# Two mixers of a four-layer block: heads' norm by four products side by side, the convolution's norm ahead of the scores, weights rounded between the first tiles

## The reference, cut to what matters

```python
xn = rmsnorm(x, norm_mix[l])
proj = xn @ w_in[l]                                   # 1024 -> 2560
u_pool, u_conv, u_diff, u_sc, u_mem = jnp.split(proj, IN_SPLITS, axis=-1)
y_pool = pool_mixer(u_pool, pool_w[l], pool_scale[l])
y_conv = conformer_conv(u_conv, conv_dw[l], conv_ln_g[l], conv_ln_b[l], conv_pw[l])
y_diff = diff_attention(u_diff, diff_qk_norm[l], diff_lambda[l], diff_subln[l], l)
y_sc = short_conv(u_sc, sconv_w[l])
y_mem = memory_attention(u_mem, mem, mem_norm[l], w_mem_kv[l], mem_qk_norm[l])
...
x = x + cat @ w_out[l]                                # cat: the five, each normed
x = x + peer_ffn(rmsnorm(x, norm_ffn[l]), ...)        # 16384 experts, dense here
```

## Time and profile before

| | |
|---|---|
| median of 3 runs | 3377.08 us (3373.78 to 3378.36) |
| profiled execution | 3372.12 us, span 3370.6 us |
| mean granted PE clock | 0.966 |
| PE busy | 3150.4 us, 93% |
| DVE, ACT, POOL busy | 1972.9, 1586.5, 274.8 us (59, 47, 8%) |
| first mixer, from the end of `plain` to the third score products | 1161.8 to 1257.2 us |

### The profile page before, as it was taken

The page is one execution under the profiler, slowest core; times in us unless marked ns, Lnnn a source line. Parts: engine busy times, 40 slices in busy tenths (PEclk is TensorE's granted clock), DMA queues, the critical chain, the costliest instruction groups (busy, mean ns, idle before and its releaser), DMA issues.

```text
span 3370.6 us, 49973 instructions
## 1 busy us (share of the span) xinstructions
PE 3150.4 (93%) x18836; PEld 2673.9 (79%) x18836; DVE 1972.9 (59%) x4121; ACT 1586.5 (47%) x3320; POOL 274.8 (8%) x376
## 2 busy tenths in 40 slices
PE   6998999998899978997999999998899789999999
PEld 3745677776699867986789999988788678999998
DVE  3233433335666556689666666656659876666665
ACT  2254322223655425319555555542541765555554
POOL 0021000000200021008000000001200620000000
PEclk9999999998999988999999999999799999999999
DMA  6502444432155423440455556543144035555554
GB/s 227 178 1 76 156 175 161 166 105 94 45 170 180 156 73 103 152 144 1 157 187 187 186 185 200 182 162 110 56 162 152 30 113 182 187 188 187 184 186 150
DMA packets 135052, 479.82 MB, mean 142 GB/s; under 512 B 15520, under 2 KB 17440, under 8 KB 134048
## 3 DMA queue, kind: packets, MB, share of 16 engines
q1 hardware_dynamic: 132944, 471.26, 42.6%
q10 hardware_dynamic: 1872, 5.38, 0.4%
HBM read 475.53 MB, written 1.05 MB: 141 GB/s over the span
## 4 chain that ended last, share of the span: by engine, by line
PE 88%; DVE 5%; ACT 3%; issue 2%; DMA 1%; POOL 0%; SPq 0%; DVEq 0%; ACTq 0%; POOLq 0%
PE psum L768 15%; PE psum L770 15%; PE psum L769 15%; PE psum L2941 7%; PE psum L2943 7%; PE psum L2942 7%; PE psum L2850 7%; PE psum L2759 4%; PE psum L863 2%; PE psum L1125 2%; PE psum L356 1%; PE psum L1135 1%; PE psum L629 1%; DMA raw<-in_mod_w 1%; DVE a_scaled L733 1%
## 5 line engine op out<-in xcount | busy, mean ns | idle before, releaser
L249 DVE TENSOR_TENSOR w_lo<-raw,w_hi 128x512 fp32r<-128x512 f32 x1424 | 958.4, 691 | 744.9 <-ACT w_hi L240 717.6
L240 ACT ACTIVATE w_hi<-raw 128x512 fp32r<-128x512 f32 x1424 | 864.4, 625 | 795.7 <-PE psum L770 419.3
L768 PE MATMUL psum<-x_hi,w_hi 128*128 128x256 f32 x1968 | 561.2, 285 | 7.7 <-issue 4.2
L770 PE MATMUL psum<-x_hi,w_lo 128*128 128x256 f32 x1968 | 558.2, 284 | 0.0
L769 PE MATMUL psum<-x_lo,w_hi 128*128 128x256 f32 x1968 | 557.7, 283 | 0.0
L2941 PE MATMUL psum<-w_hi,wt_hi 128*128 128x512 f32 x1024 | 406.9, 397 | 6.5 <-DVE wt_lo L3005 6.5
L2943 PE MATMUL psum<-w_hi,wt_lo 128*128 128x512 f32 x1024 | 406.4, 397 | 0.0
L2942 PE MATMUL psum<-w_lo,wt_hi 128*128 128x512 f32 x1024 | 405.8, 396 | 0.0
L768 PEld LDWEIGHTS psum<-x_hi,w_hi 128*128 128x128 f32 x1968 | 373.5, 190 | 17.6 <-issue 9.0
L769 PEld LDWEIGHTS psum<-x_lo,w_hi 128*128 128x128 f32 x1968 | 376.1, 191 | 7.9
L770 PEld LDWEIGHTS psum<-x_hi,w_lo 128*128 128x128 f32 x1968 | 375.1, 191 | 0.0
(11 more groups left out here) (336 smaller groups left out, 4439.0 us busy)
## 6 DMA issues: line engine op xcount, KB each, us to landing
raw<-in_v SPq DMA_DIRECT2D x256, 512.0 KB, 4.4
raw<-in_u SPq DMA_DIRECT2D x190, 512.0 KB, 3.4
raw<-in_mod_w SPq DMA_DIRECT2D x96, 512.0 KB, 4.4
raw<-in_w_gate_up SPq DMA_DIRECT2D x88, 512.0 KB, 5.2
u_raw<-in_u SPq DMA_DIRECT2D x66, 512.0 KB, 3.5
raw<-in_w_in SPq DMA_DIRECT2D x40, 512.0 KB, 3.5
raw<-in_w_down SPq DMA_DIRECT2D x32, 512.0 KB, 3.5
raw<-in_w_peer SPq DMA_DIRECT2D x32, 512.0 KB, 4.2
```

The costliest lines, as they stand in the source:

```text
L240: self.nc.scalar.activation(self.hi[:, m % 4, :], self.half(m), ACT.Copy).then_inc(self.rounded[m % 4], 1)
L249: self.nc.vector.tensor_tensor(self.lo[:, m % 4, :], self.half(m), self.hi[:, m % 4, :], ALU.subtract).then_inc(self.ready[m % 4], 1)
L768: pe.matmul(out[:, 0:width], hi[:, w], x_hi, start=(c == 0), stop=False)
L770: mm = pe.matmul(out[:, 0:width], lo[:, w], x_hi, start=False, stop=(c == total - 1))
```

## The change

The heads' norm becomes a class of its own. The squares of a set of 128x512 are now the moving operand; the weights are 32 columns of 1/n by group (`means`), and the four sets write partitions 0 to 31, 32 to 63 and so on of one bank. One square root on ACT, one reciprocal on DVE of 128x512; then four products over 32 rows each (`back`) spread set s into a bank of its own. The matrices are an input of their own (`head_mats`, 128x192), fetched with the mixer's small tensors. The first turn goes between the two tiles of `mem_values`, the second, in bank 7, behind `second`'s first tile, together with the root. `ln`'s root and inversion go between `third`'s tiles, its spread ahead of the attention's first scores, and its application ahead of the first maxima. ACT and DVE round three halves of `first` behind `plain`'s second tile. The fetch of the mixer's small tensors is now waited for by DVE, POOL and PE. Nothing of the computed values is left out.

```diff
+class HeadNorm:
+    def __init__(self, k, items, mats, banks):
+        self.means, self.back = [mats[:, 0:32], mats[:, 32:64]], mats[:, 64:64 + P]
...
+        self.root = flat(k.spread[:, 0:4, :])
+        self.sums = k.bank[6].use(written=4)
+        self.inv = [k.bank[b].use() for b in banks]
...
+    def scalar_squares(self, after):
+        for s in (0, 2):
+            act.activation(self.k.sq[:, s, :], self.items[s][0], ACT.Square).then_inc(self.by_scalar.sem, 1)
+    def vector_squares(self, after):
+        for s in (1, 3):
+            dve.tensor_tensor(self.k.sq[:, s, :], x, x, ALU.mult).then_inc(self.by_vector.sem, 1)
+    def tensor_sums(self):
...
+        for s in range(4):
+            pe.matmul(use.tensor[self.rows(s), :], self.means[s // 2], self.k.sq[:, s, :], start=True,
+                      stop=True).then_inc(use.written.sem, 1)
+    def scalar_root(self):
+        act.wait_ge(*use.full(4))
+        act.activation(self.root, use.tensor[:], ACT.Sqrt, bias=self.k.eps[:, 0:1]).then_inc(use.read.sem, 1)
+    def vector_invert(self):
+        dve.wait_ge(*self.sums.emptied())
+        dve.reciprocal(self.root, self.root).then_inc(self.inverted.sem, 1)
+    def tensor_spread(self):
...
+        for s, use in enumerate(self.inv):
+            pe.matmul(use.tensor[:], self.back[self.rows(s), :], self.root[self.rows(s), :], start=True,
+                      stop=True).then_inc(use.written.sem, 1)
+    def vector_apply(self):
+        for (x, gain), use in zip(self.items, self.inv):
+            dve.wait_ge(*use.full())
+            dve.scalar_tensor_tensor(out=x, in0=x, scalar=gain, in1=use.tensor[:], op0=ALU.mult,
+                                     op1=ALU.mult).then_inc(use.read.sem, 1)
 class TurnRows:
-    def __init__(self, k, dst, src, n, arrive):
+    def __init__(self, k, dst, src, n, arrive, bank=6):
 class MixerPlain
     def scalar_between(self, n):
+        if n == 1:
+            self.mixer.k.ring.round(0)
     def vector_between(self, n):
+        if n == 1:
+            self.mixer.k.ring.remain(0)
 class MixerMemory
+    def tensor_between(self, n):
+        if n == 0:
+            self.mixer.rows[0].tensor()
+        if n == 1:
+            hold(self.mixer.k.nc.tensor, self.mixer.fetch.done)
+            self.mixer.heads.tensor_sums()
     def scalar_between(self, n):
         self.mixer.k.ring.round(0)
+        if n == 0:
+            self.mixer.rows[0].scalar()
+            self.mixer.heads.scalar_squares(self.mixer.heads_there())
     def vector_between(self, n):
+        if n == 0:
+            self.mixer.heads.vector_squares(self.mixer.heads_there())
         self.mixer.branches.vector_taps(16 + 4 * n, 20 + 4 * n)
         self.mixer.k.ring.remain(0)
 class MixerSecond
+    def tensor_between(self, n):
+        if n == 0:
+            self.mixer.rows[1].tensor()
+    def scalar_between(self, n):
+        if n == 0:
+            self.mixer.rows[1].scalar()
+            self.mixer.heads.scalar_root()
     def vector_between(self, n):
+        if n == 2:
+            self.mixer.heads.vector_invert()
         self.mixer.branches.vector_taps(24 + 2 * n, min(26 + 2 * n, Branches.TAPS))
 class MixerThird
     def scalar_between(self, n):
+        if n == 2:
+            self.mixer.ln.scalar_root()
     def vector_between(self, n):
+        if n == 2:
+            self.mixer.ln.vector_invert()
 class MixerSteps
     def tensor_start(self):
-        self.mixer.ln.tensor_spread()
         self.mixer.branches.tensor()
 class Mixer
+        head_mats = k.sb("head_mats", [P, 64 + P], 137952)
     def tensor(self):
         self.mem_values.tensor()
-        for rows in self.rows:
-            rows.tensor()
-        self.heads.tensor_sums()
         self.second.tensor()
         self.heads.tensor_spread()
         self.third.tensor()
+        self.ln.tensor_spread()
         self.att.tensor()
     def scalar(self):
-        for rows in self.rows:
-            rows.scalar()
-        self.heads.scalar_squares(self.first.done + self.proj_done + self.memory.done + self.mem_values.done)
         self.second.scalar()
-        self.heads.scalar_root()
+        k.warm(ACT.Sqrt)
         self.third.scalar()
         ring.limit = self.beyond()
-        self.ln.scalar_root()
     def vector(self):
-        self.heads.vector_squares(self.first.done + self.proj_done + self.memory.done + self.mem_values.done)
+        hold(dve, self.fetch.done)
...
         self.second.vector()
-        self.heads.vector_invert()
         dve.wait_ge(*self.lam_made.after(2))
         self.third.vector()
         ring.limit = self.beyond()
+        self.ln.vector_apply()
         self.att.vector_first()
-        self.ln.vector_invert()
-        self.ln.vector_apply()
     def gpsimd(self):
         self.branches.clear(self.start)
+        hold(k.nc.gpsimd, self.fetch.done)
         self.branches.gpsimd_pool(self.second.done)
```

More of the change, by code:

```diff
@@ L684, in vector_apply, with rows @@
                 dve.tensor_tensor(pair[1], dst, pair[0], ALU.subtract).then_inc(self.lo.sem, 1)
+class HeadNorm:
+    def __init__(self, k, items, mats, banks):
+        self.k, self.items = k, items
+        self.means, self.back = [mats[:, 0:32], mats[:, 32:64]], mats[:, 64:64 + P]
+        self.by_scalar = k.named("heads_squared_by_scalar").take(2)
+        self.by_vector = k.named("heads_squared_by_vector").take(2)
+        self.root = flat(k.spread[:, 0:4, :])
+        self.sums = k.bank[6].use(written=4)
+        self.inverted = k.named("heads_inverted").take(1)
+        self.inv = [k.bank[b].use() for b in banks]
+        self.done = [use.emptied() for use in self.inv]
+    def rows(self, s):
+        return slice(32 * s, 32 * s + 32)
+    def scalar_squares(self, after):
+        act = self.k.nc.scalar
+        hold(act, after)
+        for s in (0, 2):
+            act.activation(self.k.sq[:, s, :], self.items[s][0], ACT.Square).then_inc(self.by_scalar.sem, 1)
+    def vector_squares(self, after):
+        dve = self.k.nc.vector
+        hold(dve, after)
+        for s in (1, 3):
+            x = self.items[s][0]
+            dve.tensor_tensor(self.k.sq[:, s, :], x, x, ALU.mult).then_inc(self.by_vector.sem, 1)
+    def tensor_sums(self):
+        pe, use = self.k.nc.tensor, self.sums
+        pe.wait_ge(*self.by_scalar.after(2))
+        pe.wait_ge(*self.by_vector.after(2))
+        pe.wait_ge(*use.free())
+        for s in range(4):
+            pe.matmul(use.tensor[self.rows(s), :], self.means[s // 2], self.k.sq[:, s, :], start=True,
+                      stop=True).then_inc(use.written.sem, 1)
+    def scalar_root(self):
+        act, use = self.k.nc.scalar, self.sums
+        act.wait_ge(*use.full(4))
+        act.activation(self.root, use.tensor[:], ACT.Sqrt, bias=self.k.eps[:, 0:1]).then_inc(use.read.sem, 1)
+    def vector_invert(self):
+        dve = self.k.nc.vector
+        dve.wait_ge(*self.sums.emptied())
+        dve.reciprocal(self.root, self.root).then_inc(self.inverted.sem, 1)
+    def tensor_spread(self):
+        pe = self.k.nc.tensor
+        pe.wait_ge(*self.inverted.after(1))
+        for use in self.inv:
+            pe.wait_ge(*use.free())
+        for s, use in enumerate(self.inv):
+            pe.matmul(use.tensor[:], self.back[self.rows(s), :], self.root[self.rows(s), :], start=True,
+                      stop=True).then_inc(use.written.sem, 1)
+    def vector_apply(self):
+        dve = self.k.nc.vector
+        for (x, gain), use in zip(self.items, self.inv):
+            dve.wait_ge(*use.full())
+            dve.scalar_tensor_tensor(out=x, in0=x, scalar=gain, in1=use.tensor[:], op0=ALU.mult,
+                                     op1=ALU.mult).then_inc(use.read.sem, 1)
@@ L2414, in __init__, with turn @@
                                           lambda t: vT[:, 1, t - 2, :], None, b0=4, between=MixerMemory(self))
-        self.rows = [TurnRows(k, rows[:].rearrange("p s (c n) -> p s c n", n=P),
-                              lambda n, j=j: vT[:, j, n % 2, (n // 2) * P:(n // 2 + 1) * P], 4,
-                              self.first.done + self.mem_values.done) for j, rows in enumerate((drow, mrow))]
+        def turn(rows, j, arrive, bank):
+            return TurnRows(k, rows[:].rearrange("p s (c n) -> p s c n", n=P),
+                            lambda n: vT[:, j, n % 2, (n // 2) * P:(n // 2 + 1) * P], 4, arrive, bank)
+        self.rows = [turn(drow, 0, self.first.done, 6), turn(mrow, 1, self.mem_values.done, 7)]
         self.proj_done = [use.emptied() for use in self.first.uses[4:6]]
@@ L2474, in tiles_done, with heads_there @@
         return [use.emptied() for use in self.plain.uses[0:n]]
+    def heads_there(self):
+        return self.first.done + self.proj_done + self.memory.done
     def sync(self):
@@ L2614, in gpsimd @@
     def gpsimd(self):
+        k = self.k
         self.memory.gpsimd()
         self.branches.clear(self.start)
+        hold(k.nc.gpsimd, self.fetch.done)
```

(6 more changed lines are left out.)

10 lines of the change are left out of this document (4 added, 6 removed).

## The result

The changed kernel takes 3322.31 us (median of 4 runs, 3320.64 to 3327.29) where the kernel before takes 3375.43 beside it (3372.26 to 3378.36): a ratio of 0.9842, 95% interval 0.9827 to 0.9856, 53.1 us less. Five more runs of it on another occasion gave 3323.97 against 3372.73 (0.9855, interval 0.9842 to 0.9869), 48.8 less. The forecast was 3328, range 3320 to 3343: faster, and inside the range.

The account below looks back on a forecast made before the run. TensorE's own order was taken as the bound, holding 88% of the chain. Terms 3.7 + 13.6 + 7.5 = 24.8 per mixer, 49.6 for both, took 3372.1 to 3322.5, 3327.5 on the median's scale; forecast 3328, range 3320 to 3343.

Parts of the forecast that it names:

- A: Weights of `first` rounded sooner: PE starts it 2.24 us earlier and at full clock, 1.5 us more; 3.7 per mixer.
- B: Values turned between tiles, heads' norm side by side: third product set effectively starts at 1213.6 instead of 1227.2; 13.6 per mixer.
- 1.7 is nearer the first, so I take it low: PE's 1.7 us wait before the heads' spread lowers the clock: spread 1.9, third product set loses 0.8 more.
- I charge 0: POOL's pooling meeting DVE's taps: POOL delayed some 3 us, but pooling wanted only at 1231, so no cost.
- The bound of strict turns: If DVE's taps and POOL's pooling exclude each other, applications end 3.4 us late and PE stands at the convolution's mean.
- with the clock kept, 15.2: Gain per mixer of the turned values and heads' norm if the clock does not fall before the spread.
- C: Convolution's norm ahead of the attention's scores: third scores start sooner after `third`; 7.5 us per mixer, bounds 6.5 and 7.9.
- the tiny addition charged with 0.4: Before the third scores, a small DVE addition may stand behind a POOL step: 0 to 0.8 us, 0.4 taken.
- rival 1: In the heads' norm little runs side by side, or POOL and DVE take turns: 10 us lost, 3337; chance 0.13.
- Rival 2: Heads' norm reciprocal dearer than its slope, 10 us say, or `second`'s 0.3 us slacks break: 3341; chance 0.09.
- 3: Nothing gained: PE's shorter path runs into weights that have not landed; 3377, chance 0.03.
- 4: Slower: the heads' norm reciprocal, with every engine behind it, undoes the gain at 28.3 us; 3390 at 35; chance 0.03.

Follow-up runs that it names:

- A undone: Changed kernel with the three halves of `first` rounded behind the plain tiles again, not behind the second one: 3332.14 us, 8.2 above the changed kernel.
- B alone: Kernel before plus only the new heads' norm and turns, without the sooner rounding or the earlier convolution's norm: 3343.58 us, 0.9916 of before.
- C undone: Changed kernel with the convolution's norm behind the attention's first scores and maxima again: 3335.64 us, 11.7 above the changed kernel; repeated, 3335.87 us.

## Why the prediction was right, point by point

**A, 3.7 per mixer.** Measured 3.8: 2.44 until `first` starts (the idle 2.09, and 0.35 by which it now overlaps the plain set's end) and 1.38 in it. The step that was too sure is "Fed without a gap it stays at full clock ... 1.5 us" as a fixed gain: without A the clock falls behind the 2.09 gap in both mixers before (0.51 and 0.53), in one of two with A undone, in neither with B alone. So 2.4 is A's certain part, and the 1.4 came in three of these six mixers; which it will be is chance as far as these runs tell.

**B, 13.6.** Measured 13.4 (from the end of `first` to the third set's start 15.6 less, and 2.2 more within that set) and 13.4 alone. The total is right, two of its terms are not, and that they cancel is luck. Sums 1.07 (taken 1.0), inversion 3.35 (taken 3.5; the slope from 16 to 512 elements is 6.3 ns, near the 6.5 of the earlier trace rows), `second` without a stall at full clock, all as forecast. Wrong: "1.7 is nearer the first, so I take it low". PE idled 1.35 and kept the clock, the spread took 1.14 for 1.9, the third set lost nothing for 0.8: 1.9 better with the shorter wait. Wrong as well: "DVE loses about one POOL step at first and then keeps its pace ... I charge 0". It lost 2.2 us in six half taps, and with 0.4 us of slack at the mean PE waited 1.87. The step drew on subtractions of the earlier trace rows that show no loss while POOL lost; which engine loses was different for the taps. The bound of strict turns was 3.4. The 0.4 of slack is luck too: the working counts all four applications and leaves out the 0.8 by which it slows the tile ahead of the mean; with pooling held back the third application, the one that PE waits for, ends 0.42 before the mean starts. The working's own value with the clock kept, 15.2, less the 1.87 gives 13.3, near the 13.4 measured. On the rule of the Trainium skill (SBUF — State Buffer, section "Who interferes with whom"), these runs agree for the taps: two SBUF inputs contend (4.68 for 2.46). An instruction with one input in SBUF and one in PSUM did not (0.74 beside POOL's additions). A single SBUF input alone is no safeguard: the copy of the earlier trace rows took 1.35 for 0.43.

**C, 7.5.** Measured 7.87 in the stretch: the tiny addition charged with 0.4 ran in 0.15 us. A neighbour paid in its place, off the path (0.77 for an L1637 step of 0.23). In the whole time both mixers' C was worth 12, not 15.7; the rest fits the clock of the attention, but that was not settled. The working's list of seven idle times leaves out an eighth, 1.06 before the pooling's product (1.05 again with C undone); as C is summed from positions, nothing hangs on it.

**The sum.** 24.8 per mixer was forecast; the two traces give 25.1 from the last plain tile to the third scores in each mixer, and 49.9 between the spans, against 49.6. By the medians it is 53.1 and 48.8. The forecast of 3328 lies 4 to 6 us above them by its base: 5.0 us were added to go from the profiled execution to a median of three runs, 3377.1, and larger sets of the same kernel gave 3372.7 to 3375.4.

**The rivals.** Of rival 1 the half with POOL came true (2.2 of 3.4), the half with nothing side by side did not; had it, the spread alone would have cost 5.5 per mixer and not the 1.6 of the working, since the clock falls with it. Rival 2's dear reciprocal fell, its rate held: 6.7 us more cost 7.3. Nothing of 3 and 4 was seen.

## What to carry to other kernels

When an engine's work moves in time, list what the *other* engines run at its new place: here POOL's pooling, which starts 10 us sooner after the start of `first` than before, landed on a kind of DVE instruction that it slows, and one extra wait for it bought 2.1 us per mixer. When a bound queue has waits at two points, reordering it only shifts the wait; look for work that fits into its idle time, and make sure that it stands ahead of the instruction that waits. And judge small edits by a stretch of the trace that repeats to 0.1 us (and look at its clock: with A undone its two mixers differ by 1.5), not by the median of a kernel whose clock makes it scatter by several.

## What the runs showed of the hardware

**The clock's scatter sits in a few places.** Unchanged code before the mixers brings `first` to 1155.76 us in one execution of the changed kernel and to 1162.26 in the other. By ACT's table loads the two are level at 20 us, 3.6 apart at 186 and 6.7 at 355, and stay so to within 0.3; from 150 to 200 us the granted clock is 0.86, then 0.93 in the one and 0.73, then 0.83 in the other. The attention takes 41.2 to 46.2 us from the third scores to the output product over all traces. The mean granted clock over it goes along, though not strictly: 0.76 and 0.79 with 41.2 and 41.4, 0.74 with 42.4, 0.70 with 43.3, 0.61 with 46.2. The Trainium skill (TensorE: Matmul & The Clock Gate, section "What's actually happening") says that the number of slow products varies from run to run of one kernel; the traces agree.

**The spread side by side kept the clock.** After the same 1.35 us of idle time the spread on four row groups ran at 1.00, the one on a single group fell to 0.62 and 0.50 and left the next tile slow: 1.14 against 6.47 us, where running one after the other alone explains 3.5.

**DVE's reciprocal costs eight copies**: 3.35 us for 128x512 against 0.42. From 16 to 512 columns that is 6.3 ns for each, where the earlier trace rows has 6.5 between 2 and 16.

**Who loses when DVE and POOL meet depends on the pair.** The taps took 1.9 times their time while POOL's first additions lost 0.13 and 0.06 of 1.09 and 1.08; in the earlier trace rows two POOL steps took 1.81 beside DVE's undisturbed subtractions.
